# Four empty blocks in a weight stream, shorter DMA rows for the weight sums, and two ScalarE instructions exchanged

## The chip, the cores and the metric

The kernel runs on one core of one Trainium2 chip. The metric is the device time of one execution in microseconds, as the median of the runs. The profile shows one further execution of the same program, taken with the hardware profiler; its engines are PE (TensorE, with its weight loads as PEld), DVE (VectorE), ACT (ScalarE), POOL (GpSimd) and SP (SyncE, which issues the weight loads).

## The reference

Sequence length 512, width 1024, everything in float32. Two layers of a first block, then two layers of a second one:

```python
for i in range(2):                      # first block
    if i == 0:
        mix = conformer_conv(x, ...)    # x @ pw1, a * sigmoid(g), 31-tap depthwise, layer_norm, silu, @ pw2
    else:                               # 16 heads of 64
        q, k, v = x @ wq, x @ wk, x @ wv
        mix = stick_breaking_attention(q, k, v) @ wo
    x = layer_norm(alpha * x + mix)
    u = x @ w_up                        # 1024 x 2816
    g = causal_dwconv(x @ w_gate, conv_w, conv_b)      # 3 taps
    ffn = (silu(g) * u) @ w_down
    ple = sigmoid(x @ ple_gate) * (p[i] @ ple_proj)
    x = layer_norm(alpha * x + ffn + ple)
for l in range(2):                      # second block
    z = rmsnorm(x) @ w_in[l]            # split into the parts of two mixers
    x = x + concat(gated_linear_attention(z), softmax_attention(z)) @ w_out[l]
```

## The kernel before, in words

**Layout and precision.** The activations lie transposed in SBUF, as eight tiles of 128 features by 512 tokens (k = 0 to 7). To keep float32's accuracy at TensorE's faster rate, each operand is split in two: a high part, rounded to fp32r by ScalarE, and a low part, the rest, which VectorE makes by subtracting (`less`, L2192 to L2194; all its instructions carry L2194). A product of a 128x128 weight block takes three matmuls into the same bank: XH by wh, XH by wl, XL by wh (`block` in the TensorE program, its matmuls all at L620). Activations are held as `X`, `XH`, `XL`; the FFN's hidden ones as `HH`, `HL`.

**The weight stream.** All weights come as one sequence of 128x128 blocks, laid out by `weight_order` (L61) in just the order in which TensorE uses them. Eight blocks (NU = 8) make a unit of 128x1024 numbers, 512 KB; there are 308 units. SyncE loads unit after unit into a ring of three raw buffers `wraw` (`raw` in `sync_program`, L547) and reuses a buffer as soon as VectorE has made the low part of the unit three before. ScalarE rounds the unit (`round_to`, L1447) and VectorE subtracts (`rest_to`, L2198), both in strict unit order, into one of four slots `wh`, `wl`. A slot is free when TensorE has passed the last block of the unit that held it; TensorE tells this by raising the semaphore `stream` at the end of each group of blocks and at the end of each unit. Each instruction stream calls `feed` or `feed_group` at the places where TensorE uses a block; where that block is the first of a unit (p % NU == 0), the engine makes the unit three further on (AHEAD = 3). So where a unit begins in the order decides where, among an engine's other work, a rounding stands and what it waits for. Some units do not use the four slots: at four places units go into space that is free at the time (`Stream.spare`, L162 to L168), so that they can be made far ahead, beside work with which TensorE is not fed yet. For layer 1 they are the units that hold wq with k = 2, 4 and 6, for the second block's first layer those that hold in0 with k = 2, 4 and 6, in each case found by the position of that block in the sequence. `None` in the sequence is an empty block: it fills a place, is loaded with the unit, and is never multiplied.

**Start of a layer.** The normalisation of the layer before runs in two halves of the tokens, and `head` (L724) follows it: TensorE goes through k = 0 to 7 with the blocks of four output tiles for tokens 0 to 255, then again for tokens 256 to 511. For layer 1 those blocks are wq and wk of columns 0 and 1, four blocks per k, so 32 in all. At present 32 blocks do not begin at a unit's start but four blocks in: unit 117 holds the last four of layer 0 and k = 0, unit 118 k = 1 and 2, unit 119 k = 3 and 4, unit 120 k = 5 and 6, unit 121 k = 7 and the first four of wv. Units 118 to 120 are the spare ones. ScalarE rounds them between the steps of the normalisation (L1792 to L1810) and after them the unit that holds wv's first block; VectorE makes the low parts in `between_last` (L2652 to L2676), the last fill of which comes after the second half's `XL`. For in0 the sequence is aligned (`align`, L66), a spare unit holds k = 2 and 3, the next k = 4 and 5, the last k = 6 and 7, and the same code runs.

**FFN.** 22 tiles of hidden features. The first 2 * PAIRS tiles (PAIRS = (3, 7): three pairs in layer 0, seven in layer 1) are computed two at a time with a scheme that takes seven products of half size in place of eight. It needs sums of weight quarters (`tu` for up, `tg` for gate, 16 blocks a pair each) and sums of the activations (`XS`). Per pair and matrix TensorE makes the first products, then 16 summed blocks in groups of four, then the last product (`first_products`, `summed_products`, `last_product`, L792 to L819). ScalarE copies partial results out of the banks (`first_out`, `second_out`), VectorE combines them (`first_combined`, `three_combined`, `last_combined`, L2391 to L2408), and between these ScalarE and VectorE finish the pair before: VectorE's three taps of the convolution, ScalarE's `silu`, VectorE's product, the high part on ScalarE, the low part on VectorE. TensorE's last product of a pair's up matrix waits for the third value of `three_combined` (`sqr` or `third` in the rows, L2185). ScalarE's order is the loop at L1583 to L1612: silu(f - 1), which needs the taps of the pair before, then `second_out(0, tu, p)`.

**Weight sums.** POOL builds tu and tg in HBM before they are needed (`weight_sums`, L3225): each of the four parts in `SUMMED` (L25) is a chain of eight DMAs from HBM to HBM into `tw`, four copies (L3219) and four that add to what lies there (L3223). A step waits for the one before it and for a number of units made by VectorE. An entry is (layer, first and last of the matrices, that number for the first step, units between steps). Parts 0 and 1 belong to layer 0, 2 and 3 to layer 1. SyncE's loads of tu and tg blocks wait for the sums.

```python
for n, (put, dst, src) in enumerate(((copy, t3, w12), (add, t3, w22), (copy, t2, t3), (add, t2, w11),
                                     (copy, t4, t2), (add, t4, w21), (copy, t1, w12), (add, t1, w11))):
    pool.wait_ge(s.w_lo, at + step * n)
    put(dst, src, done + n)
```

**Around the change in the stream.** In `ffn_order` (L45) layer 0's pairs begin with a filler of four empty blocks for the gate blocks that a first pair doesn't have. Behind them the sequence ends layer 0 four blocks off a unit's start, so that `wq`, `wo` and layer 1's `up` begin in the middle of a unit, while layer 1's first `tu` block begins one (layer 0's first `tu` block stands in a unit's middle). The output projection takes wo with k = 0 to 4 for eight columns, then k = 5 and 6 for three columns and k = 7 last, beside the last heads of the attention (L1078 to L1090, L1888 to L1899). Unit 147 begins at the block of wo with k = 6 and column 1.

Of the kernel before, what the change touches and what calls it, by code (L numbers as in the profile page):

```python
# [5 lines left out]
ALU = mybir.AluOpType  # L6
# [15 lines left out]
ALPHA = 4.0 ** 0.25  # L22
PAIRS = (3, 7)

SUMMED = [(0, 0, 4, 16, 1), (0, 4, 6, 38, 1), (1, 0, 6, 60, 4), (1, 6, 14, 100, 5)]  # L25
XS0 = 14
TAPS = 31

# [16 lines left out]
def ffn_order(layer):  # L45
    out = []
    for p in range(PAIRS[layer]):
        f, (up, gate), (tu, tg) = 2 * p, (f"up{layer}", f"gate{layer}"), (f"tu{layer}", f"tg{layer}")
        out += [(up, k, f) for k in range(KD)]
        out += [(gate, k, f - 1) for k in range(4, KD)] if p else [None] * 4  # L50
        out += [(tu, k, p) for k in range(16)] + [(gate, k, f) for k in range(KD)]
        out += [(up, k, f + 1) for k in range(4, KD)] + [(tg, k, p) for k in range(16)]
    f = 2 * PAIRS[layer]
    out += [(f"up{layer}", k, f) for k in range(KD)] + [(f"gate{layer}", k, f - 1) for k in range(4, KD)]
    out += [(f"gate{layer}", k, f) for k in range(KD)]
    for f in range(2 * PAIRS[layer] + 1, FT):
        out += [(f"up{layer}", k, f) for k in range(KD)] + [(f"gate{layer}", k, f) for k in range(KD)]
    return out
# [1376 lines left out]
def scalar_program(act, m, s, w, nc):  # L1435
# [97 lines left out]
    def ffn(layer, i):  # L1533
        HH = m.HH[layer]
        for f0 in (0, 4):
            if f0:
                feed_group(f"pg{layer}", range(KD), range(f0, f0 + 4))
            for c in range(f0, f0 + 4):
                act.wait_ge(s.stream, w.done(f"pg{layer}", KD - 1, c))
                if c >= 4:  # L1540
                    act.wait_ge(s.pg_x, 8 * layer + c - 3)
                fn(tmp[c % 4][:, :], bank[c][:, :], ACT.Sigmoid).then_inc(s.pg_u, 1)
            if f0 == 0:
                for j in range(4):
                    act.wait_ge(s.xs_f, 4 * layer + j + 1)
                    fn(m.XS[layer][j][:, :, 0:256], m.SF[layer][j], ACT.Copy).then_inc(s.xs_h, 1)
        up, gate, tu, tg = f"up{layer}", f"gate{layer}", f"tu{layer}", f"tg{layer}"

        def bias(f, g):

            act.wait_ge(s.pg_x, 8 * layer + 8)
            if f >= 2:
                act.wait_ge(s.f_h, FT * layer + f - 1)
            fn(tmp[2 * f % 4][:, :], g[:, :], ACT.Identity, scale=P(f"fcw{layer}", 3 * f + 2), bias=P(f"fcb{layer}", f)).then_inc(s.f_u, 1)

        def silu(f):

            u = tmp[2 * f % 4]
            act.wait_ge(s.f_conv, FT * layer + f + 1)
            fn(u[:, :], u[:, :], ACT.Silu).then_inc(s.f_silu, 1)  # L1560

        def high(f):

            act.wait_ge(s.f_h, FT * layer + f + 1)
            fn(HH[:, f, :], tmp[(2 * f + 1) % 4][:, :], ACT.Copy).then_inc(s.f_hi, 1)

        def pair_bias(p, odd):
            act.wait_ge(s.u_c, combined(layer, p, 1, 4 + odd))
            bias(2 * p + odd, m.gb[odd])

        def first_out(g, mat, p):
            if g == 0 and p >= 2:
                act.wait_ge(s.f_h, FT * layer + 2 * p - 2)
            act.wait_ge(s.stream, w.done(mat, KD - 1, 2 * p))
            fn((m.ub[layer][p], m.gb)[g][0][:, 0:256], bank[3 * g][:, 0:256], ACT.Copy).then_inc(s.u_e, 1)

        def second_out(g, mat, p):
            if g == 0 and p:
                act.wait_ge(s.f_h, FT * layer + 2 * p - 1)
            act.wait_ge(s.stream, w.done(mat, 15, p))  # L1580
            fn((m.ub[layer][p], m.gb)[g][1][:, 0:256], bank[3 * g][:, 0:256], ACT.Copy).then_inc(s.u_e, 1)

        for p in range(PAIRS[layer]):  # L1583
            f = 2 * p
            if p:
                second_out(1, tg, p - 1)
            feed_group(up, range(KD), [f])
            if p:
                pair_bias(p - 1, 0)
            first_out(0, up, p)  # L1590
            if p:
                feed_group(gate, range(4, KD), [f - 1])
            feed_group(tu, range(4), [p])
            if p:
                pair_bias(p - 1, 1)
            feed_group(tu, range(4, 12), [p])
            if p:
                silu(f - 2)
            feed_group(tu, range(12, 16), [p])
            feed_group(gate, range(4), [f])  # L1600
            if p:
                silu(f - 1)
            second_out(0, tu, p)
            feed_group(gate, range(4, KD), [f])
            feed_group(up, range(4, KD), [f + 1])
            if p:
                high(f - 2)
            first_out(1, gate, p)
            feed_group(tg, range(8), [p])
            if p:  # L1610
                high(f - 1)
            feed_group(tg, range(8, 16), [p])  # L1612
        last = PAIRS[layer] - 1
        second_out(1, tg, last)
        for f in range(2 * PAIRS[layer], FT):
            feed_group(up, range(KD), [f])
            if f == 2 * PAIRS[layer]:
                pair_bias(last, 0)
                feed_group(gate, range(4, KD), [f - 1])
                pair_bias(last, 1)  # L1620
                silu(f - 2)
                silu(f - 1)
                high(f - 2)
                high(f - 1)
            feed_group(gate, range(KD), [f])
            act.wait_ge(s.stream, w.done(gate, KD - 1, f))
            bias(f, bank[gate_bank(f)])
            silu(f)
            high(f)
        table(LNEXP)  # L1630
        for c in range(7):
            feed_group(f"down{layer}", range(FT), [c])
            square(i + 1, c, X[:, c, :])
# [1569 lines left out]
def gpsimd_program(pool, m, s, a):  # L3203
    C = m.C

    def tt(o, i0, i1, op):
        return pool.e.tensor_tensor(o, i0, i1, op)

    def add_sum(i, c, x0, x):
        pool.wait_ge(s.xsum, 8 * i + c + 1)  # L3210
        if c == 1:
            pool.wait_ge(s.nrm_u, 8 * part_at(i))
        else:
            pool.wait_ge(s.accs, acc_at(i) + c - 1)
        tt(m.acc_s[:, :], x0 if c == 1 else m.acc_s[:, :], x, ALU.add).then_inc(s.accs, 1)

    def copy(dst, src, after):
        pool.wait_ge(s.tw, 16 * after)
        pool.e.dma_start(dst, src).then_inc(s.tw, 16)  # L3219

    def add(dst, src, after):
        pool.wait_ge(s.tw, 16 * after)
        pool.e.dma_start(dst, src, accum_op=ALU.add, max_dma_last_dim=8192).then_inc(s.tw, 16)  # L3223

    def weight_sums(part):  # L3225

        layer, n0, n1, at, step = SUMMED[part]
        t1, t3, t4, t2 = (a["tw"][t, layer, n0:n1].rearrange("n p c -> (n p) c") for t in range(4))
        w11, w12, w21, w22 = (a[n][layer, n0:n1].rearrange("n p c -> (n p) c") for n in ("w11", "w12", "w21", "w22"))
        done = 8 * part  # L3230
# [5 lines that stand above are left out]
    for i in (1, 3):  # L3236
        for part in ((0,), (1, 2, 3))[i // 2]:
            weight_sums(part)
        for c in range(1, KD - 1 if i == 3 else KD - TAIL[i] - SPLIT[i]):
            add_sum(i, c, m.X[:, 0, :], m.X[:, c, :])  # L3240
        for h in range(2 if SPLIT[i] else 0):
            for c in range(KD - TAIL[i] - SPLIT[i], KD - TAIL[i]):
                if h:
                    pool.wait_ge(s.xsum, 8 * i + c + 1)
                else:
                    pool.wait_ge(s.xa, half_at(i + 1) + c - KD + 1)
                pool.wait_ge(s.accs, acc_at(i) + c - 1 + (SPLIT[i] + FIRST_TAIL[i]) * h)
                v = m.acc_s[:, tokens(i, h)]
                tt(v, v, m.X[:, c, tokens(i, h)], ALU.add).then_inc(s.accs, 1)
    for layer in range(2):  # L3250
        pool.wait_ge(s.v0, layer + 1)
        for i in range(2):
            pool.e.memset(m.states[:, i, 0, :], 0.0).then_inc(s.st0, 1)
# [161 lines left out]
```

## Time and profile before

| | |
|---|---|
| runs | 1762.31, 1762.95 and 1764.30 us; median 1762.95 |
| profiled execution | 1766.01 us, its span 1764.2 us |
| granted TensorE clock, mean | 0.995 |
| busy shares | PE 98%, PEld 81%, DVE 65%, ACT 51%, POOL 2% |
| moved by DMA | 213.75 MB, 121 GB/s |

The span is what the engines' records cover; the execution's own time is 1.8 us longer. Times are counted from the start of the span. The brackets at a row give the idle time of that engine just before it and what ended it. PEclk is the clock granted to TensorE as a fraction of 2.4 GHz; 0.50 is 1.2 GHz. The stages in the trace: the convolution layer to about 230 us, layer 0's FFN behind it, layer 1 from 639 on with attention and the output projection to about 900, then its FFN with the seven pairs from about 960 to 1110, and the second block from about 1306 on.

### The profile page before, as it was taken

The numbers are of one execution on the slowest core, as the hardware profiler recorded it, in microseconds if no ns is written. First come the engines' busy times: TensorE is split into PE (matmuls) and PEld (weight loads), VectorE is DVE, ScalarE is ACT, GpSimd is POOL, SyncE is SP. The second block draws the span as 40 slices with busy tenths as digits, with TensorE's granted clock in tenths as the row PEclk, the third lists the DMA queues.
The fourth block names the chain that finished last, engine by engine and source line by source line (L and its number), as shares of the span: only waits on it lengthen the run. The fifth ranks groups of instructions, "written<-read, shape, count | busy, mean of one in ns | idle before, by whom it ended". The sixth has DMA issues, their size and how long they took to land.

```text
span 1764.2 us, 24404 instructions
## 1 busy us (share of the span) xinstructions
PE 1729.5 (98%) x9933; PEld 1436.1 (81%) x9933; DVE 1150.0 (65%) x1813; ACT 897.4 (51%) x1409; POOL 40.0 (2%) x53
## 2 busy tenths in 40 slices
PE   9999999999999979999999999999999999999999
PEld 7877998888888878777778999888898877778766
DVE  6779887644433453887687887543368866656674
ACT  6789655433332353666564565432255454534542
POOL 0000100000000000000020000000000000000000
PEclk9999999999999989999999999999999999999999
DMA  5374256755446536311114555233223222132111
GB/s 214 132 207 117 96 168 198 243 167 167 133 142 199 136 112 187 96 51 58 63 64 155 174 178 169 95 96 107 96 72 105 93 63 66 67 96 96 60 60 48
DMA packets 59808, 213.75 MB, mean 121 GB/s; under 512 B 7088, under 2 KB 7344, under 8 KB 56752
## 3 DMA queue, kind: packets, MB, share of 16 engines
q1 hardware_dynamic: 56240, 170.25, 29.4%
q0 software_dynamic: 3456, 41.95, 9.0%
q8 instruction: 78, 1.28, 0.3%
q14 instruction: 34, 0.28, 0.0%
HBM read 207.97 MB, written 44.04 MB: 143 GB/s over the span
## 4 chain that ended last, share of the span: by engine, by line
PE 79%; DVE 10%; ACT 6%; DMA 2%; issue 2%; SPq 0%; ACTq 0%; DVEq 0%
PE bank L620 78%; DVE tmp L2185 3%; DVE wl L2194 2%; ACT tmp L1439 2%; ACT wh L1439 1%; DMA wraw<-in_wstream 1%; DMA wraw<-tw 1%; DVE XL L2194 1%; ACT taps L1439 1%; DVE tmp L2182 1%; DVE HL L2194 1%; DVE sqr L2185 1%; PE bank L1384 0%; ACT X L1439 0%; DVE HH L2194 0%
## 5 line engine op out<-in xcount | busy, mean ns | idle before, releaser
L2194 DVE TENSOR_TENSOR wl<-wraw,wh 128x1024 fp32r<-128x1024 f32 (+1 forms) x295 | 357.4, 1220 | 304.6 <-ACT wh L1439 303.5
L620 PE MATMUL bank<-XH,wh 128*128 128x512 f32 (+1 forms) x1424 | 527.9, 371 | 14.2 <-DVE wl L2194 11.8
L620 PE MATMUL bank<-XL,wh 128*128 128x512 f32 (+1 forms) x1424 | 517.7, 364 | 0.0
L620 PE MATMUL bank<-XH,wl 128*128 128x512 f32 (+1 forms) x1424 | 517.7, 364 | 0.0
L1439 ACT ACTIVATE wh<-wraw 128x1024 fp32r<-128x1024 f32 (+1 forms) x295 | 309.1, 1054 | 362.2 <-PE bank L620 318.4
L620 PEld LDWEIGHTS bank<-XH,wh 128*128 128x128 f32 x1424 | 269.7, 189 | 67.9 <-issue 20.2
L620 PEld LDWEIGHTS bank<-XH,wl 128*128 128x128 f32 x1424 | 269.6, 189 | 43.1
L620 PEld LDWEIGHTS bank<-XL,wh 128*128 128x128 f32 x1424 | 270.0, 190 | 39.6 <-issue 0.7
L620 PE MATMUL bank<-HL,wh 128*128 128x256 f32 (+1 forms) x740 | 215.4, 333 | 9.2 <-DVE sqr L2185 7.9
L620 PE MATMUL bank<-HH,wh 128*128 128x256 f32 (+1 forms) x740 | 216.2, 334 | 0.1
L620 PE MATMUL bank<-HH,wl 128*128 128x512 f32 (+1 forms) x580 | 199.8, 345 | 0.0
L620 PEld LDWEIGHTS bank<-HL,wh 128*128 128x128 f32 x740 | 130.2, 192 | 24.7 <-DVE sqr L2185 9.4
L620 PEld LDWEIGHTS bank<-HH,wh 128*128 128x128 f32 x740 | 130.0, 191 | 14.1 <-DVE Y L2185 0.6
L620 PEld LDWEIGHTS bank<-HH,wl 128*128 128x128 f32 x580 | 110.4, 190 | 13.1
L1439 ACT ACTIVATE tmp<-tmp 128x512 f32<-128x512 f32 (+2 forms) x131 | 72.1, 591 | 66.1 <-DVE tmp L2182 65.6
L1439 ACT ACTIVATE tmp<-bank 128x512 f32<-128x512 f32 (+4 forms) x129 | 70.3, 566 | 16.1 <-PE bank L620 14.0
L2185 DVE TENSOR_TENSOR X<-X,bank 128x512 f32<-128x512 f32 (+1 forms) x58 | 38.5, 666 | 41.8 <-PE bank L620 41.7
L2182 DVE SCALAR_TENSOR_TENSOR tmp<-bank,prm,tmp 128x511 f32<-128x511 f32 (+1 forms) x48 | 35.9, 749 | 44.3 <-ACT tmp L1439 43.5
L1439 ACT ACTIVATE tmp<-bank,prm 128x512 f32<-128x512 f32 (+1 forms) x44 | 30.5, 696 | 56.3 <-PE bank L620 56.0
L620 PE MATMUL bank<-XH,HL 128*128 128x256 f32 x256 | 57.6, 287 | 0.3 <-DVE XL L2194 0.2
L620 PE MATMUL bank<-wh,XH 128*128 128x512 f32 x128 | 50.7, 396 | 0.1
L1439 ACT ACTIVATE sqr<-X 128x512 f32<-128x512 f32 (+1 forms) x41 | 23.2, 567 | 52.7 <-DVE X L2185 48.4
(383 smaller groups left out, 2438.9 us busy)
## 6 DMA issues: line engine op xcount, KB each, us to landing
wraw<-in_wstream SPq DMA_DIRECT2D x257, 512.0 KB, 3.6
wraw<-tw SPq DMA_DIRECT2D x80, 256.0 KB, 3.0
tw<-in_w POOLq DMA_DIRECT2D x6, 1536.0 KB, 10.9
tw<-in_w POOLq DMA_DIRECT2D x4, 2048.0 KB, 16.4
wraw<-in_wstream SPq DMA_DIRECT2D x22, 256.0 KB, 3.1
tw<-in_w POOLq DMA_DIRECT2D x4, 1024.0 KB, 10.5
tw<-in_w POOLq DMA_DIRECT2D x6, 512.0 KB, 6.7
tw<-tw POOLq DMA_DIRECT2D x2, 1536.0 KB, 7.9
```

Of the source, the lines that this page charges most:

```text
L620: return pe.e.matmul(o, l, r, start=start, stop=stop, skip_group_check=True)
L1439: return act.e.activation(o, i, f, **kw)
L2182: return dve.e.scalar_tensor_tensor(out=o, in0=i0, scalar=sc, in1=i1, op0=op0, op1=op1)
L2185: return dve.e.tensor_tensor(o, i0, i1, op)
L2194: return dve.e.tensor_tensor(o, x, h.bitcast(F32), ALU.subtract)
```

## The change

The gate blocks of the first tile behind the pairs are followed by four empty blocks, in both layers. The stream becomes 309 units long (2472 blocks, with 2464 before), and every block behind layer 0's pairs moves by four, every block behind layer 1's pairs by eight in all. In the ScalarE program's loop over the pairs the copy of the second product is put ahead of silu(f - 1). The weight sums' DMAs, copies and adds, get rows of at most 4096 bytes (max_dma_last_dim; the adds had 8192, the copies none), and parts 0 and 1 of the weight sums begin one and two units earlier.

```diff
--- before.py
+++ after.py
@@ -22,7 +22,7 @@
 ALPHA = 4.0 ** 0.25
 PAIRS = (3, 7)
 
-SUMMED = [(0, 0, 4, 16, 1), (0, 4, 6, 38, 1), (1, 0, 6, 60, 4), (1, 6, 14, 100, 5)]
+SUMMED = [(0, 0, 4, 15, 1), (0, 4, 6, 36, 1), (1, 0, 6, 60, 4), (1, 6, 14, 100, 5)]
 XS0 = 14
 TAPS = 31
 
@@ -52,7 +52,7 @@
         out += [(up, k, f + 1) for k in range(4, KD)] + [(tg, k, p) for k in range(16)]
     f = 2 * PAIRS[layer]
     out += [(f"up{layer}", k, f) for k in range(KD)] + [(f"gate{layer}", k, f - 1) for k in range(4, KD)]
-    out += [(f"gate{layer}", k, f) for k in range(KD)]
+    out += [(f"gate{layer}", k, f) for k in range(KD)] + [None] * 4
     for f in range(2 * PAIRS[layer] + 1, FT):
         out += [(f"up{layer}", k, f) for k in range(KD)] + [(f"gate{layer}", k, f) for k in range(KD)]
     return out
@@ -1598,9 +1598,9 @@
                 silu(f - 2)
             feed_group(tu, range(12, 16), [p])
             feed_group(gate, range(4), [f])
+            second_out(0, tu, p)
             if p:
                 silu(f - 1)
-            second_out(0, tu, p)
             feed_group(gate, range(4, KD), [f])
             feed_group(up, range(4, KD), [f + 1])
             if p:
@@ -3216,11 +3216,11 @@
 
     def copy(dst, src, after):
         pool.wait_ge(s.tw, 16 * after)
-        pool.e.dma_start(dst, src).then_inc(s.tw, 16)
+        pool.e.dma_start(dst, src, max_dma_last_dim=4096).then_inc(s.tw, 16)
 
     def add(dst, src, after):
         pool.wait_ge(s.tw, 16 * after)
-        pool.e.dma_start(dst, src, accum_op=ALU.add, max_dma_last_dim=8192).then_inc(s.tw, 16)
+        pool.e.dma_start(dst, src, accum_op=ALU.add, max_dma_last_dim=4096).then_inc(s.tw, 16)
 
     def weight_sums(part):
```

## Rows read from the trace of the kernel before

**Rows 1.** Page, part 1: busy time, share of the span, instructions of each engine.

```profile
PE 1729.5 (98%) x9933; PEld 1436.1 (81%) x9933; DVE 1150.0 (65%) x1813; ACT 897.4 (51%) x1409; POOL 40.0 (2%) x53
```

**Rows 2.** Timeline of PE (start us, us, instruction, [idle before <-releaser]), start of layer 1.

```profile
638.92 0.55 PE L620 MATMUL bank<-XH,wh 128*128 128x256 f32 x1 [9.95 <-DVE wl L2194]
```

**Rows 3.** Timeline of PE, four of the pairs' last products.

```profile
289.55 0.80 PE L620 MATMUL bank<-HL,wh 128*128 128x256 f32 x2 [3.70 <-DVE sqr L2185]
...
984.42 0.50 PE L620 MATMUL bank<-HL,wh 128*128 128x256 f32 x2 [1.42 <-DVE sqr L2185]
...
1005.44 0.50 PE L620 MATMUL bank<-HL,wh 128*128 128x256 f32 x2 [0.61 <-DVE third L2185]
...
1089.57 0.50 PE L620 MATMUL bank<-HL,wh 128*128 128x256 f32 x2 [0.61 <-DVE sqr L2185]
```

**Rows 4.** Timeline of ACT and PE, output projection of layer 1.

```profile
877.89 1.06 ACT L1439 ACTIVATE wh<-wraw 128x1024 fp32r<-128x1024 f32 x1 [6.70 <-PE bank L620]
...
880.86 0.50 PE L620 MATMUL bank<-OH,wh 128*128 128x512 f32 x1 [1.71 <-DVE OL L2194]
```

**Rows 5.** Convolution stage: its window (columns under Rows 7), and a row of ACT's timeline.

```profile
100.00:200.00 100.00, 96.27 (x709) 80.94 (x708) 83.51 (x132) 83.02 (x136) 11.09 (x12) 1.00 0.54 160
...
114.02 1.06 ACT L1439 ACTIVATE HH<-wraw 128x1024 fp32r<-128x1024 f32 x1 [3.24 <-DMA wraw<-in_wstream]
```

**Rows 6.** Timeline of ACT and DVE, start of layer 1 (x3: merged with two rows behind).

```profile
631.74 1.04 ACT L1439 ACTIVATE wh<-wraw 128x1024 fp32r<-128x1024 f32 x1
...
637.55 3.49 DVE L2194 TENSOR_TENSOR wl<-wraw,wh 128x1024 fp32r<-128x1024 f32 x3
```

**Rows 7.** Windows: busy us of PE, PEld, DVE, ACT, POOL; PEclk, DMA share, GB/s.

```profile
630.00:640.00 10.00, 1.08 (x5) 1.11 (x6) 8.46 (x19) 8.37 (x15) 0.00 (x0) 0.65 0.02 6
...
640.00:650.00 10.00, 10.00 (x74) 10.00 (x74) 1.04 (x1) 0.00 (x0) 0.00 (x0) 0.84 0.42 153
...
1306.00:1310.00 4.00, 3.68 (x28) 3.37 (x27) 3.91 (x9) 3.46 (x8) 0.00 (x0) 1.00 0.33 129
```

**Rows 8.** Chain of waits (start us, us, what).

```profile
260.78 7.69 DMA wraw<-in_wstream
...
274.26 8.18 DMA wraw<-tw
...
880.86 16.99 PE bank L620 x70
...
1005.44 14.68 PE bank L620 x120
```

**Rows 9.** Windows, attention stage of layer 1.

```profile
700.00:800.00 100.00, 99.16 (x574) 75.28 (x573) 81.99 (x172) 69.83 (x139) 0.89 (x1) 1.00 0.26 71
```

**Rows 10.** Timeline of ACT and DVE, third pair of layer 1.

```profile
1003.57 0.63 ACT L1439 ACTIVATE tmp<-tmp 128x512 f32<-128x512 f32 x1 [0.46 <-DVE tmp L2182]
...
1004.11 0.37 ACT L1439 ACTIVATE third<-bank 128x256 f32<-128x256 f32 x1
...
1004.51 0.42 DVE L2185 TENSOR_TENSOR sqr<-third,bank 128x256 f32<-128x256 f32 x1 [0.97 <-ACT third L1439]
```

**Rows 11.** DMA view of 220 to 290 us (queue: packets, MB, share); last row: whole kernel.

```profile
q0 software_dynamic: 448, 4.19, 23.5%
...
wraw<-in_wstream SPq DMA_DIRECT2D x6, 512.0 KB, 4.8
...
wraw<-in_wstream SPq DMA_DIRECT2D x257, 512.0 KB, 3.6
```

**Rows 12.** Timeline of POOL: two issues of the weight sums.

```profile
247.54 0.78 POOL L3223 DMA_DIRECT2D tw<-in_w  x1 [8.25 <-DVE wl L2194]
...
273.64 0.78 POOL L3223 DMA_DIRECT2D tw<-in_w  x1 [4.48 <-DMA tw<-in_w]
```

**Rows 13.** Windows, PE alone (busy us, PEclk, DMA share, GB/s), behind the 3.70 us.

```profile
290.00:294.00 4.00, 4.00 (x21) 0.50 0.41 134
...
294.00:298.00 4.00, 4.00 (x31) 0.87 0.80 239
```

## The prediction

> **What bounds the kernel now.** I read the page's busy shares first: TensorE's matmuls fill 1729.5 us, 98% of the span [rows 1]. The change adds and removes no matmul, so only the 34.7 us in which PE is idle can move, and what PE loses at half clock after an idle stretch. The next view is PE's timeline, searched for rows with idle time in brackets. One is large: 9.95 us before 638.92 [rows 2]. The others within reach are 3.70 before 289.55, 1.42 before 984.42 and 0.61 or 0.62 before each of five pairs from 1005.44 to 1089.57 [rows 3], 1.71 before 880.86 [rows 4], and 3.73 in all between 100 and 200 us [rows 5]. The question at each is which wait ends last, and whether the change touches it.
>
> **The padding, at the head of layer 1.** The stream stands four blocks off there: units 118 to 120 are the spare ones, rounded early, but wq and wk of k = 7 stand in unit 121, with wv 0. PE goes through k = 0 to 7, first for tokens 0 to 255. VectorE makes unit 121's low part only after the whole normalisation (the last fill of `between_last`): at 637.55, its high part having been made at 631.74 [rows 6]. So PE stops at 629, at k = 7 of the first half. With four blocks of padding 118 is an ordinary unit and 119 to 121 are the spare ones with k = 2 to 7. That is the order which the in0 stage has today, in the same code: there PE is busy 3.68 of 4 us where its normalisation starts [rows 7], 0.32 lost. The second half's XL rows come late, but they end by 637.6 [rows 6]; a k takes PE twelve matmuls of 0.122 (120 in 14.68 us [rows 8]), 1.46 us, and starting the second half at about 630 it reaches k = 7 at 640. Nothing is late next. Gain: 9.95, and the clock. PEclk 0.84 over 640 to 650 is 3.2 us at 1.2 GHz in place of 2.4 [rows 7]; with the 1.08 before 640 that is 4.3 us at half speed, 2.1 lost. **12.0 us**, bounds 8 and 12.3.
>
> **The padding, elsewhere.** The stream grows from 308 to 309 units: one more load and rounding, 1.04 us of ScalarE and 1.16 of VectorE [rows 6], beside PE, 0. If that cover is gone they cost 2.2 once. In the attention stage ScalarE's rounding moves from k = 4 of a matrix to k = 0, ahead of the next scores. PE is busy 99.16 of 100 us there [rows 9]. I take 0, with bounds of one rounding, -1 and +1.
> In the output projection unit 147 starts now at wo 6,1. ScalarE's round for it waits until PE has finished wo 6,0, and it stands ahead of the last head's copy: it comes at 877.89 after 6.70 us of idle time, and PE waits 1.71 for OL [rows 4]. After the shift the unit starts at wo 5,0 and the round waits for wo 4,7, four blocks earlier, twelve matmuls of 0.24 (70 in 16.99 [rows 8]), 2.9 us, more than the stall. **1.7**, bounds 0 and 1.7.
> From layer 1's own padding on, the stream is today's moved by a whole unit: 0.
>
> **The second copy ahead of the second silu.** In each pair ScalarE runs silu(f-1), which waits for VectorE's taps, at 1003.57, and then the copy of the second product at 1004.11; VectorE's three combinations follow from 1004.51 [rows 10], and PE's last product starts at 1005.44 when the second one is done. That second product was finished long before: eight blocks of 0.37 lie between it and the waiting one. Copied first, it lets the combinations start when the taps end, at about 1003.55, 1.0 us sooner. The stall is 0.61, so all of it goes; five times, and the 1.42 of the second pair, where ScalarE also loads a table: 4.5. silu(f-1) slips by the copy, 0.37 [rows 10]; behind it VectorE's product and the high part are wanted only a pair later. Layer 1's pairs also get layer 0's alignment, in which no unit starts at gate k = 0, so that one feed less stands between. **4.3**, bounds 2.5 and 4.7.
>
> **The weight sums and layer 0's pairs.** The 3.70 us before 289.55 come from loads: in the chain of waits stand a load of 7.69 us at 260.78 and one of 8.18 at 274.26 [rows 8]; the median is 3.6 over the kernel and 4.8 in this stretch [rows 11]. Beside them run POOL's sums, step 3 of part 1 at 247.54 and step 7 at 273.64, 6.5 us a step [rows 12], in packets of 9.4 KB (4.19 MB in 448 [rows 11]). With the threshold two units lower, step 5 stands where step 3 did and step 7 at 260.6: this traffic ends near 267, not 280. The load at 274 then costs what the median does, 4.6 less, and with the reorder's 1.0 the chain through load, table, silu and taps is early enough. PE gains 3.70, and the clock behind it: PEclk 0.50 and 0.87 [rows 13] with the 0.45 before 290 are 5.5 us at 1.2 GHz, 2.7 lost at most. Bounds: 1.0 (the reorder alone) and 6.4. Nearest is layer 1's second pair, without sums beside it, which loses 1.42 in the old order and less than the reorder and alignment give back in the new one. **5.4**.
> No row prices the shorter rows. A load meets packets of 9.4 KB now; at 4 KB its wait for a turn should halve. Against it, queue 0's packets more than double; if each cost what it does now, its share of 23.5% [rows 11] would pass 50%. Their own effect lies between -2 and +2 us.
> The Trainium skill's page "DMA: Bandwidth & Descriptors" (Queues, rings and completion order) says that an engine takes turns between queues by whole packets of several descriptors. By that rule shorter rows give nothing unless the packet shrinks with them; the sum would be 1.4 us smaller. No row here tells a packet from a descriptor.
> In the convolution stage ScalarE, which paces it, waited 3.24 us for a load at 114.02 [rows 5], while part 0 moves its data. PE's 3.73 us of idle time hang on ScalarE. Part 0 starts a unit earlier, which shifts its steps against the loads and doesn't clear them. Bounds -2 and 3.0; **1.4**, for the shorter turns.
>
> **Sum.** 12.0 + 1.7 + 4.3 + 5.4 + 1.4 = 24.8 us. The profiled execution took 1766.0 (span 1764.2), 3.1 over the median of the runs, 1762.95. Against it this is 1741.2, against the median **1738**.
>
> **Rivals.**
> *The DMA parts give nothing:* the earlier sums meet other loads. Against it: they do leave 267 to 280. Then 1.4 goes and 5.4 becomes 1.0: 24.8 - 5.8 = 19.0, **1744**.
> *Row size is indifferent, only the thresholds work* (the packet rule's case): 1.4 goes and a third of layer 0's: 21.6, **1741**.
> *The head of layer 1 keeps part of its wait:* XL's second half or wv's first unit ends last in place of unit 121; 3 to 5 us stay with some of the clock, **1743**. Against it: the in0 stage.
> *Slower:* the sums come too late. Layer 0's third pair reads part 1. A pair takes 21.0 us ((1089.57 - 1005.44) / 4 [rows 3]), its sums are multiplied from the middle on and loaded three units (8.8 us) ahead, so none is wanted before about 289.55 + 10.5 - 8.8, say 290. Three steps remain after 247.54: done at 267, 23 us to spare. It bites when smaller rows double a step to 14 us; at 24 us a step the sums end at 319.5, PE waits 29.5, and the kernel takes 1738 + 29.5 = **1767.5**. Packets that each cost what they do now would make a step at most 2.3 times as long (9.4 / 4), 15 us, and the sums end at 292.5, 2.5 late.
> *It doesn't do what it says:* the spare units could fall on other blocks and unit 121's wait stay. Worked out from the order, they move along.
>
> **Numbers.** Forecast 0.60 (its own range 1733 to 1742), no gain from DMA 0.14, rows indifferent 0.12, part of the head's wait left 0.09, slower 0.03, nothing 0.02. All but the last two are faster: 0.95. A measurement of this kernel tells 0.2%, 3.5 us, from no change. Range 1733 to 1746: the low end has 3.0 in the convolution stage, 6.4 in layer 0 and one rounding in attention (24.8 + 1.6 + 1.0 + 1.0, and the shorter rows' own 1.6 at most); the high end is the first rival with two roundings in the way.
>
> **What would show it.** Right: no idle row of 10 us near 630; PE's last product of layer 1's pairs without idle time from the third on, the copy to `third` or `sqr` ahead of the silu; no idle time before wo 7; POOL's last add of part 1 at about 260; loads beside the sums at 3 to 4 us; over 10,000 packets on queue 0. Wrong: a new PE row waiting for wl behind DMA wraw<-tw, half clock anywhere between 300 and 1700, sums of part 1 ending after 290. The forecast falls if the head of layer 1 isn't shorter by 11 us or more, for that is half of the sum.

## The result and the profile after

The changed kernel took 1736.62 us (median of four runs, 1735.42 to 1736.95), the kernel before 1762.63 beside it; the ratio is 0.9851, with a 95% interval of 0.9838 to 0.9863. That is 26.0 us less. The forecast was 1738 (24.8 us less), in a range of 1733 to 1746. The same kernel in a later set of runs took 1740.04 (below, the run of the change again), so the eight runs together have a median of 1736.9.

The page after: the busy shares, the granted clock in 40 slices, and the DMA queues.

```profile
span 1735.0 us, 24407 instructions
...
PE 1722.2 (99%) x9933; PEld 1430.8 (82%) x9933; DVE 1149.9 (66%) x1814; ACT 898.0 (52%) x1410; POOL 42.7 (2%) x53
...
PEclk9999999999999999999999999999999999999999
...
q1 hardware_dynamic: 56384, 170.77, 30.2%
q0 software_dynamic: 10752, 41.95, 9.6%
...
wraw<-in_wstream SPq DMA_DIRECT2D x258, 512.0 KB, 3.6
```

As many matmuls as before [rows 1], PE's busy time 7.3 us shorter, the span 29.2 us shorter. The 7.3 are put down to what the idle stretches had cost in clock and in pipelining, since the matmuls are the same. Queue 0, on which the weight sums run, has three times its packets for the same bytes.

PE's timeline after, the rows with idle time between 200 and 1300 us (the rows left out between them have no idle time).

```profile
206.36 0.38 PE L620 MATMUL bank<-XH,HL 128*128 128x256 f32 x1 [0.20 <-DVE XL L2194]
...
264.68 0.50 PE L620 MATMUL bank<-HL,wh 128*128 128x256 f32 x2 [1.39 <-DVE sqr L2185]
...
609.80 0.39 PE L620 MATMUL bank<-XH,wh 128*128 128x256 f32 x1 [0.25 <-DVE XL L2194]
...
688.17 0.50 PE L620 MATMUL bank<-XH,wh 128*128 128x512 f32 x1 [0.30 <-DVE OH L2182]
...
816.87 0.50 PE L620 MATMUL bank<-OH,wh 128*128 128x512 f32 x1 [0.26 <-DVE X L2182]
...
837.82 0.50 PE L620 MATMUL bank<-OH,wh 128*128 128x512 f32 x1 [0.26 <-DVE X L2182]
...
1278.25 0.39 PE L620 MATMUL bank<-XH,wh 128*128 128x256 f32 x1 [0.32 <-DVE XL L2182]
```

The 9.95 us of [rows 2], the 3.70, 1.42 and five times 0.6 of [rows 3] and the 1.71 of [rows 4] have no counterpart. All idle rows of PE together fall from 30.9 us to 9.2. One row is worse: 1.39 at 264.68, where the kernel before had 0.51.

Windows after (busy us of PE, PEld, DVE, ACT, POOL; PEclk, DMA share, GB/s): layer 1's start, what follows layer 0's third pair, and 100 us of attention, which answer to [rows 7], [rows 13] and [rows 9].

```profile
620.00:630.00 10.00, 10.00 (x86) 10.00 (x85) 8.49 (x23) 8.82 (x18) 0.00 (x0) 1.00 0.01 2
284.00:288.00 4.00, 4.00 (x36) 4.00 (x35) 4.00 (x7) 3.36 (x6) 0.00 (x0) 1.00 0.20 71
690.00:790.00 100.00, 100.00 (x588) 76.56 (x587) 81.20 (x170) 69.21 (x140) 1.16 (x1) 1.00 0.28 74
```

PE's granted clock is 1.00 there: 36 matmuls in 4 us behind the third pair, where there were 21 and 31.

ScalarE and VectorE in layer 1's third pair after, to be held against [rows 10], and POOL's last step of part 1, against [rows 12].

```profile
977.26 0.38 ACT L1439 ACTIVATE third<-bank 128x256 f32<-128x256 f32 x1 [0.38 <-PE bank L620]
977.67 0.42 DVE L2185 TENSOR_TENSOR sqr<-third,bank 128x256 f32<-128x256 f32 x1
977.76 0.63 ACT L1439 ACTIVATE tmp<-tmp 128x512 f32<-128x512 f32 x1
978.13 0.42 DVE L2185 TENSOR_TENSOR third<-bank,sqr 128x256 f32<-128x256 f32 x1
```

```profile
260.16 0.81 POOL L3223 DMA_DIRECT2D tw<-in_w  x1 [3.95 <-DMA tw<-in_w]
```

The copy to `third` stands ahead of the silu, the combinations begin with no idle time when the taps end (977.67), and the one that PE wants is done at 978.55, 1.3 us before PE's last product at 979.88. The last step of part 1 lands 8.44 us after its issue, at 268.6.

ScalarE's rounding ahead of the last head's copy, against [rows 4]:

```profile
852.69 1.06 ACT L1439 ACTIVATE wh<-wraw 128x1024 fp32r<-128x1024 f32 x1 [2.40 <-PE bank L620]
```

**Where the 29.2 us of the two spans went.** The same row of PE is found in both timelines, and the difference of the start times is read: 0.4 us is gained by 9.7 us (before the sums begin), 1.2 by 207, 7.1 at 617 (609.80), 19.7 at 708 (688.17), 20.5 at 837 (816.87), 29.2 at 1307 (1278.25) and at the end. So: start and convolution 1.2, layer 0's FFN 5.9, layer 1's start 12.1 with 0.5 of the first attention stall behind it, the rest of attention 0.7, and 8.7 from there to the second block. The profiled execution of before stood 3.4 us over the median beside it (1766.0 and 1762.63), that of after 0.2 over its own; this is why 29.2 us of span are 26.0 in the medians. From the row at 617 to the end it is 1147.3 us before and 1125.2 after, 22.1 less, and 1125.2 to 1126.2 in all nine profiles that have the padding. What lies ahead of that row differs from execution to execution, as the experiments show.

### The profile page after: what moved, and what is told of

It reads as the page before. It is cut to its first block, busy times and chain, and to the rows that moved or that the text cites. A ratio compares the mean times of both kernels' runs of the same rounds, so it can differ in the third digit from the quotient of the medians.

```text
span 1735.0 us, 24407 instructions
## 1 busy us (share of the span) xinstructions
PE 1722.2 (99%) x9933; PEld 1430.8 (82%) x9933; DVE 1149.9 (66%) x1814; ACT 898.0 (52%) x1410; POOL 42.7 (2%) x53
## 3 DMA queue, kind: packets, MB, share of 16 engines
q0 software_dynamic: 10752, 41.95, 9.6%
## 4 chain that ended last, share of the span: by engine, by line
PE 89%; DVE 5%; ACT 4%; DMA 1%; issue 1%; SPq 0%; DVEq 0%; ACTq 0%
PE bank L620 88%; ACT tmp L1439 1%; DMA wraw<-in_wstream 1%; DVE wl L2194 1%; DVE tmp L2185 1%; ACT wh L1439 1%; ACT taps L1439 1%; PE bank L1384 0%; DVE XL L2194 0%; DVE sbl L2194 0%; DVE HL L2194 0%; ACT Y L1439 0%; ACT XH L1439 0%; DVE X L2182 0%; DVE sqr L2185 0%
## 5 line engine op out<-in xcount | busy, mean ns | idle before, releaser
L620 PE MATMUL bank<-wh,XL 128*128 128x512 f32 x128 | 49.9, 390 | 0.0
```

The costliest lines, as they stand in the source:

```text
L620: return pe.e.matmul(o, l, r, start=start, stop=stop, skip_group_check=True)
```

## The experiments

Twelve runs of kernels (the ninth is the change itself), in three sets of four, each set on a chip of its own; each set shares its runs of the kernel before. The first four take the change apart.

**e1, the padding alone.** The `[None] * 4` of the diff and nothing else.

> The padding alone, everything else as before. The idle 9.95 us at layer 1's start and its half clock (12.3 us together by the two profiles) and the 1.71 us ahead of wo with k = 7 go; of layer 1's pairs the theory, which gives their gain to the exchange of the copy and silu, expects the stalls to stay at 0.5 to 0.7 us each: 12.3 + 1.5 = 13.8 us, ratio 0.9922. Rival: the shift of unit starts alone clears the pairs' stalls (before, a unit starts at the gate's k = 0, ahead of the copy): 13.8 + 6.4 = 20.2 us, ratio 0.9885. Layer 0's pairs and the convolution stage lie ahead of the padding: nothing there by either.

Measured: 1740.4 us (1738.69 to 1745.68) against 1762.61, ratio 0.9883 (0.9866 to 0.99): 22 us by the medians, 21 by the ratio. The rival holds. PE's timeline, the last product of layer 1's second pair and of the third:

```profile
962.48 0.51 PE L620 MATMUL bank<-HL,wh 128*128 128x256 f32 x2 [0.40 <-DVE sqr L2185]
...
982.74 0.40 PE L620 MATMUL bank<-HL,wh 128*128 128x256 f32 x2
```

The third has no idle time, with silu still ahead of the copy. ScalarE has silu at 980.62, the copy at 981.16, and the combinations start at 981.56. From silu's start to PE's turn it is 2.1 us, where it was 1.1 before (1003.57 [rows 10] to 1004.67): the order is the old one, and it is a microsecond earlier against PE. Where the microsecond comes from stands in VectorE's timelines, before (first row) and with the padding alone (second row). It is the low part that VectorE makes ahead of the product and the taps for which silu waits:

```profile
1000.26 1.23 DVE L2194 TENSOR_TENSOR wl<-wraw,wh 128x1024 fp32r<-128x1024 f32 x1 [1.16 <-ACT wh L1439]
...
977.32 1.23 DVE L2194 TENSOR_TENSOR wl<-wraw,wh 128x1024 fp32r<-128x1024 f32 x1 [0.57 <-ACT wh L1439]
```

It starts 4.4 us ahead of PE's turn before and 5.4 with the padding. Its rounding, the one that ScalarE does ahead of silu(f - 2), had waited 0.48 us for PE (999.17), and with the unit starting four blocks earlier it waits for PE no more (976.24). The rounding at the gate's k = 0 (1002.05) was not what held silu back before: it had ended 0.46 us earlier [rows 10].

**e2, the exchange alone.**

```diff
+            second_out(0, tu, p)
             if p:
                 silu(f - 1)
-            second_out(0, tu, p)
```

> The exchange of copy and silu alone. Theory: 0.6 to 0.8 us in each of layer 1's pairs from the third on and 1 us of the second pair's 1.42, about 4.5 us, and 1.0 us or more in layer 0's third pair, with what of the clock comes back: 5 to 8 us in all, ratio 0.9955 to 0.997. Rival (a unit starts at the gate's k = 0 with the old alignment, and its rounding still stands ahead of the copy and waits for a bank or a load): the stalls stay, 0 to 1 us. Second rival for layer 0: its 3.70 us come from silu's table and taps, and the copy alone clears them, then PE shows no half clock at 290 though the sums still run late.

Measured: 1755.72 us (1754.84 to 1759.1) against 1762.61, ratio 0.997 (0.9959 to 0.9981): 5 to 7 us, the theory's own case. PE's timeline, layer 0's second pair, layer 1's second, and layer 1's third:

```profile
266.37 0.80 PE L620 MATMUL bank<-HL,wh 128*128 128x256 f32 x2 [3.49 <-DVE sqr L2185]
...
978.50 0.50 PE L620 MATMUL bank<-HL,wh 128*128 128x256 f32 x2 [0.36 <-DVE sqr L2185]
...
998.76 0.40 PE L620 MATMUL bank<-HL,wh 128*128 128x256 f32 x2
```

Layer 1's stalls go here too. From the first pair's last product to the seventh's it is 127.0 us in the kernel before (962.58 to 1089.57), 121.6 with the padding alone, 121.7 with the exchange alone and 121.0 with both. **The two edits cure the same stall**: 5.4 and 5.3 alone, 6.0 together. In layer 0 a stall of 3.49 stands at the second pair in place of the third: it wanders from execution to execution.

**e3, the shorter rows alone**, and **e4, the lower thresholds alone** (both as in the diff).

> Rows of 4096 bytes alone, thresholds as before. Theory (a load waits for the turn of a packet of the sums, and this one is half as long): loads beside the sums go from 4.7 to below 4 us in the median, the convolution stage gains 1 us, layer 0's third pair 1 to 3 us: 1 to 4 us, ratio 0.998 to 0.9995. Rival (only when the sums run matters, not how their rows are cut): the medians stay at 4.7 us and the ratio is 0.9995 to 1.0005. Packets on queue 0 are near 10,750 by both.

> Thresholds of parts 0 and 1 lower by one and two units alone. Theory: part 1 ends near 267 us in place of 280, the loads at 274 cost their median and layer 0's third pair loses at most 1 us in place of 3.70, with the clock behind it 3 to 6 us gained; convolution stage within 0.5 us: ratio 0.9965 to 0.998. Rival (the reorder or the rows are needed for it): under 1 us, ratio above 0.9994.

Measured: rows 1762.75 us (1760.73 to 1767.63), ratio 1.0008 (0.9997 to 1.0018); thresholds 1761.73 us (1758.39 to 1766.96), ratio 0.9996 (0.9985 to 1.0006). Neither is told from no change; the medians of the times are those of the rivals (the rows' ratio lies just past its 1.0005). The single profiles say more. DMA view of 220 to 290 us, thresholds alone, and PE's row at layer 0's third pair:

```profile
wraw<-in_wstream SPq DMA_DIRECT2D x6, 512.0 KB, 3.9
```

```profile
284.78 0.50 PE L620 MATMUL bank<-HL,wh 128*128 128x256 f32 x2 [0.40 <-DVE sqr L2185]
```

And with the rows alone:

```profile
wraw<-in_wstream SPq DMA_DIRECT2D x6, 512.0 KB, 4.4
```

```profile
271.74 0.50 PE L620 MATMUL bank<-HH,wh 128*128 128x256 f32 x2 [1.27 <-DVE acc_s L2185]
...
289.54 0.80 PE L620 MATMUL bank<-HL,wh 128*128 128x256 f32 x2 [3.15 <-DVE sqr L2185]
```

The median load (of six) is 3.9 and 4.4 us, against 4.8 [rows 11], and the stall of 3.70 becomes 0.40 and 3.15. What the thresholds gain in layer 0 in this profile (403.3 us from PE's row at 207 to that at 617, 409.3 before) the timed runs don't show in full; why, the later sets tell in part.

**e5, one unit earlier, without padding.** ScalarE rounds unit 121 behind the first half's last tile, VectorE subtracts it there:

```diff
-            elif h == 1 and f == 3:
+            elif h == 0 and f == 7:
                 round_to(w.at["wv", 0, 0] // NU)
...
                 between(i, mat, t)
+                if i == 2 and t == 7:
+                    rest_to(w.at["wv", 0, 0] // NU)
```

> The stream as before, without padding; only unit 121 (wq and wk of k = 7, wv 0) is rounded and subtracted earlier, behind the first half's normalisation in place of after the second. Theory (PE's 9.95 us wait for that one unit's low part): PE then has k = 7 at about 630 us, the idle row falls under 1 us and the clock stays up, 11 to 12.3 us gained, ratio 0.993 to 0.994, while the stalls of wo and of layer 1's pairs stay as they were. Rival (the second half's XL or a later unit ends next): 3 to 5 us stay, gain 5 to 8 us, ratio 0.9955 to 0.997.

Measured: 1751.8 us (1750.66 to 1754.06) against 1762.74, ratio 0.9938 (0.9926 to 0.9951): 11 us. VectorE's timeline and the window in which PE had been busy for 1.08 us before [rows 7]:

```profile
627.26 1.22 DVE L2194 TENSOR_TENSOR wl<-wraw,wh 128x1024 fp32r<-128x1024 f32 x1
```

```profile
630.00:640.00 10.00, 10.00 (x86) 10.00 (x85) 8.53 (x20) 8.38 (x15) 0.00 (x0) 1.00 0.14 50
```

So the stall at layer 1's start hangs on one unit's low part, 1.22 us of VectorE's work 10 us too late, and PE has no idle row of 0.2 us or more from there to 695.70. From 616.66 to the first attention stall (695.70) it is 79.0 us, 91.0 before, 78.4 with the padding. The other stalls (0.84, 0.99, 1.71, and 0.6 in the pairs) are all in this trace, at their old size: they don't hang on unit 121. The first three are in e2's trace too, so of the change's parts only the padding can have taken them.

**e6, the change without the exchange**, and **e7, the change without both edits of the sums.**

> The change without the exchange of copy and silu. If the shifted unit starts clear layer 1's pairs by themselves, as the run with padding alone says, only layer 0's third pair can lose something: 1737 to 1739 us, ratio to before 0.9855 to 0.9865. If the exchange is worth what the prediction gives it (4.3 us in layer 1): 1741 us, ratio 0.988.

> The change without shorter rows and earlier thresholds: padding and exchange alone. The prediction's sum without its 1.4 us of the convolution stage and with 1.0 in place of 5.4 in layer 0's pairs would be 1742.4. By the single runs of rows and thresholds (within 0.2% of before) it is 1736 to 1739 us, ratio 0.985 to 0.9865, with a wider spread of the runs than the change's own 1.5 us, since loads meet the sums at other moments each time.

Measured: 1740.31 us (1738.72 to 1744.65), ratio 0.9875 (0.9859 to 0.9892), and 1740.83 us (1738.89 to 1741.6), ratio 0.9873 (0.9859 to 0.9886). Both lie between the two values expected of each, and about 4 us over the change's first; whether that is the parts or the set of runs, e9 was to tell. In e6 the stretch from 837 to the second block takes 462.1 us, 461.4 in the change: the exchange is worth 0.7 us in layer 1 once the padding is in, not the 4.3 of the prediction.

**e8, a version beyond the change.** In layer 0's second pair the copy waits behind a rounding, and the rounding for a load. The copy is put ahead of it:

```diff
                 silu(f - 2)
+            second_out(0, tu, p)
             feed_group(tu, range(12, 16), [p])
             feed_group(gate, range(4), [f])
-            second_out(0, tu, p)
```

> The change, and the copy of the up matrix's second product put ahead of the rounding at the summed block 12 too, where in layer 0's second pair the copy waits for a rounding that waits for a load (the change's profile loses 1.39 us there at 264.68). Theory: that stall goes, 0.5 to 1.4 us gained in layer 0, layer 1 as it was: 1735.5 to 1736.5 us, ratio to before 0.985. Rival: the rounding behind the copy comes late by the copy's wait and PE waits for its low part: a new row waiting for wl in each pair, 0.5 us or more times ten, 1741 us.

Measured: 1739.94 us (1738.69 to 1740.99), ratio 0.9871 (0.9856 to 0.9887): not the 1735.5 to 1736.5 of the theory. PE waits for no wl in any pair, and layer 0 from 209.65 to 611.58 takes 401.9 us, the shortest of all profiles. But the convolution stage lost it again, to a load of 8.75 us at 121.32 in the chain of waits:

```profile
134.64 0.80 PE L620 MATMUL bank<-cinh,HH 32*128 32x512 f32 x4 [4.20 <-DVE cinl L2194]
```

**e9, the change again**, the scale for the three that follow.

> The changed kernel once more, so that the next three runs can be held against it on the same chip. In the runs of the change on record it took 1735.4 to 1737.0 us; other chips gave 1739 to 1741 for kernels that lack one part each. If those parts are worth what lies between, this one comes to 1736.6 again; if it is the chip or the day, it comes to 1738 to 1740 and the three parts (exchange, both of the sums' edits) are worth 1 to 2 us at the most.

Measured: 1740.04 us (1736.67 to 1743.26) against 1761.99, ratio 0.9879 (0.9858 to 0.9899). The same program, and its runs spread over 6.6 us. So e6, e7 and e8 can't be told from the change by their medians, and neither can the padding alone: e1's 22.2 us and 0.9883 stand beside 22.0 and 0.9879 here. What the exchange and the sums add to the padding is seen in the profiles and in the change's first four runs, not in this set. Its profiled execution took 1743.3, 6.4 us more than the change's first; of these 2.9 arise before the row at 207, 3.4 between it and the row at 617, 0.1 behind. Two rows of PE carry it, with ScalarE's wait in front of the second.

```profile
134.54 0.80 PE L620 MATMUL bank<-cinh,HH 32*128 32x512 f32 x4 [3.72 <-DVE cinl L2194]
...
269.65 0.80 PE L620 MATMUL bank<-HL,wh 128*128 128x256 f32 x2 [3.41 <-DVE sqr L2185]
```

```profile
260.92 0.82 POOL L3223 DMA_DIRECT2D tw<-in_w  x1 [4.68 <-DMA tw<-in_w]
261.04 0.80 SPq L561 DMA_DIRECT2D wraw<-tw  x2
...
267.36 1.06 ACT L1439 ACTIVATE wh<-wraw 128x1024 fp32r<-128x1024 f32 x1 [7.15 <-DMA wraw<-tw]
268.32 0.37 ACT L1439 ACTIVATE sqr<-bank 128x256 f32<-128x256 f32 x1
```

POOL issues the last sum of part 1 at 260.92, SyncE a unit's loads 0.12 us later, and ScalarE gets that unit after 7.15 us; the copy stands behind the rounding, and PE waits 3.41. Loads of such length stood in the chain of [rows 8] too. From layer 1's start on nothing of the kind is seen: the stretch from 617 to 837 takes 207.0 to 207.1 us in all nine profiles with the padding, and the one from 1307 to the end 456.7 to 456.8 in all fourteen.

**e10, part 0 at its old threshold; e11, the change with the old rows; e12, e8 with part 0 at its old threshold.**

> The change, but part 0 of the weight sums at its old threshold (16); part 1 keeps the new one (36). By the profiles so far layer 0's pairs take 403 to 404 us from 207 on with the lower thresholds and 407 to 410 without, and the stretch up to 207 takes 206.4 to 209.7 with them and 204.1 to 207.6 without. Theory: part 1's threshold gives all of the gain in layer 0 and part 0's costs something in the convolution stage, where it starts earlier and ends among the same loads: 0.5 to 2 us less than the change. Rival: part 0's place is indifferent and the differences up to 207 us are chance: within 0.5 us of the change.

> The change with the rows of the sums' DMAs as before (8192 bytes in the adds, uncut in the copies). Theory, by the run of rows alone (1.0008 of before, 0.9997 to 1.0018): the row size is indifferent, within 1 us of the change. Rival (shorter rows help only once the sums are moved): 1 to 3 us slower than the change, in the convolution stage, with the loads' median beside the sums above 4.6 us.

> A version meant to beat the change: the copy of the second product ahead of the rounding at summed block 12, and part 0 of the sums at 16. The copy alone took layer 0's pairs from 403.4 to 401.9 us by the profiles. Theory: 1.5 us from that, and what part 0's old threshold gives (0 to 2 us): 1.5 to 3 us below the change. Rival: the differences are lost in the spread of the loads, within 1 us of the change.

Measured, against 1761.99: e10 1739.51 us (1735.35 to 1741.99), 0.9873 (0.9851 to 0.9896); e11 1739.84 us (1737.01 to 1744.04), 0.988 (0.9859 to 0.9901); e12 1736.78 us (1735.97 to 1737.11), 0.9859 (0.9842 to 0.9877). The old rows cost nothing that shows beside e9. Part 0's threshold is not told apart by the runs. e12 is 3.3 us under e9 in the median and its runs keep within 1.1 us; the intervals overlap, and the change's own first runs had a median within 0.2 us of it (1736.62), so it isn't shown to beat the change. Its profile speaks against a version without late loads: ScalarE waits 5.51 us for a load before 267.52, PE 1.78 for `acc_s` at 270.23, and layer 0 takes 403.9 us, where 401.9 were expected from e8.

**All fourteen profiles together** say what single medians can't (the fourteenth is the kernel before). From PE's row at about 207 us to that at about 617:

| thresholds of the sums | layer 0's FFN, us | mean |
|---|---|---|
| part 1 at 38 (before, e1, e2, e3, e5, e7) | 409.3, 407.4, 406.8, 408.7, 410.3, 407.8 | 408.4 |
| part 1 at 36 (change, e4, e6, e8 to e12) | 403.4, 403.3, 404.0, 401.9, 406.8, 403.8, 402.9, 403.9 | 403.8 |

Up to the row at 207 us it takes 206.0 in the mean of the eight profiles with part 0 at 16 (204.1 to 207.6), and 207.7 in the mean of the six with part 0 at 15 (206.4 to 209.7). Part 1's earlier start gives 4.6 us, with one exception among fourteen (e9, for the reason above, which reaches the lowest of the other row); part 0's seems to cost 1.7, in ranges that overlap. Together 2.9 us; the timed runs of e4 gave 0.7, with an interval that reaches to 2.6 and takes in no gain at all. Between e7, which lacks both edits of the sums, and the change it is 0.8 by the second set of runs and 4.2 by the first. The size of the sums' part thus stays open between nothing and some 4 us.

## Why the prediction was right, and where not

**The head of layer 1: right.** 12.0 us forecast, 12.1 by the two timelines, 11 in e5's medians for the unit alone. The step "that is the order which the in0 stage has today" carried it: 0.32 us are lost at in0 [rows 7], and from 609.80 to 688.17 PE has no idle row at all. The second half's XL did not end last; the rival fell.

**The output projection: right.** 1.7 forecast; from PE's row before it (857.79 and 837.82) to the one at the old stall (880.86 and 859.04) the difference grows by 1.85. ScalarE's rounding is 5.2 us earlier against PE than before (852.69 and 877.89, with 19.97 between the two timelines), more than the 2.9 of the prediction.

**The pairs of layer 1: the mechanism was right, the term too small and given to the wrong edit.** "The stall is 0.61, so all of it goes; five times": the six periods fell by 6.0 us and not by 4.3, beyond the bound of 4.7. A bracket of 0.61 isn't what a stall costs. PE issues a matmul of this form every 0.12 us, while the row shows 0.28 for each; ahead of 1005.44 the last one starts at 1004.55, so the next is 0.77 late against its turn, and the pair's first weight block loses another 0.10. The period falls from 21.03 to 20.16, by 0.87 for 0.61 of idle time. And the alignment, which the sentence on it counts as one feed less, was worth the whole: either edit alone gives nearly all. It works by another unit than the prediction names: not by the feed at gate k = 0, but by the rounding and low part ahead of the taps, which come a microsecond earlier (e1). Counted one after the other, the exchange adds 0.7 behind the padding.

**Attention: taken at 0.** It gave 0.5 and 0.7 at the first stalls (0.84 to 0.30, 0.99 to 0.26) and lost 0.5 at a new one at 837.82, so 0.7 net, within the bounds of 1. That the padding moves these stalls is shown: the nine profiles with it have the new sizes, e5 and the others without it the old ones. That ScalarE's rounding at k = 0 in place of k = 4 is the reason is argued only.

**Layer 0 and the weight sums: the mechanism is borne out by the profiles, the size open.** "This traffic ends near 267": the last add stands at 260.16 and lands at 268.6, and PE's stall at layer 0's third pair is 0.53 us at the most in the eight profiles with the lower threshold, and 1.16 to 4.41 in five of the six without it (e2 has none). 5.4 forecast, 5.9 between the two profiles, 4.6 from the thresholds by all profiles, 0.7 from e4's timed runs. The exchange's 1.0 is neither shown nor refuted: without the lower thresholds e2 and e7 average 407.3 and the four others 408.9, in ranges that overlap. Its working at the stall held as well: from 271 us, where the two timelines differ by 0.8, to 295, where they differ by 7.1, it is 6.3 us for a stall of 3.70 and the clock behind it, against 6.4 at most. What the step missed is the second pair: there the copy is behind a rounding that is behind a load, hence 1.39 at 264.68 and 3.41 in e9. The move of the sums didn't bring this about. Before, a step stood at nearly the same time (260.81), and e2 and e1, with the old thresholds, lose 3.49 and 1.38 at the second pair.

**The convolution stage: not supported.** "1.4, for the shorter turns": the profiles' 1.2 up to 207 us have 0.4 before the sums begin, and shorter rows change nothing in e3 (1.0008) and e11 (0.988 beside 0.9879). Part 0's earlier start has, if anything, the other sign. The rival "row size is indifferent, only the thresholds work" is what the runs support; its price was small.

**The sum: near in part by luck.** Against the profiled execution it said 1741.2; after took 1736.8. Of the 4.4 us between, layer 1's pairs are 2.4 (1.7 in the six periods, 0.7 at the first pair's 0.47, which had no term), attention 0.7, layer 0 0.5, the output projection and the wl row behind it 0.4; the rest is under 0.5. Against the medians the sum is 1.2 us short, since before's profiled execution was a long one and the sum took its stalls as typical. Two errors of opposite sign also meet in it. From 617 us on the terms come to 18.0 (12.0, 1.7 and 4.3), where all profiles with the padding show 21 to 22; ahead of that they come to 6.8 (5.4 and 1.4), of which the timed runs of rows and thresholds alone show next to nothing. The change's second set, 22.0 us under before, fits 22 from layer 1 on and almost nothing ahead of it; the first set, 26.0, had more ahead. Both lie in the range.

**The slower rival** wanted a step of 24 us; after, part 1's copies and adds land in 4.3 and 7.4 us in the median beside layer 0's FFN and end near 267, far from 290.

## What to carry to other kernels

When a stream of fixed units feeds an engine, look at which unit the first consumer of a stage stands in: four blocks in the wrong unit cost 12 us here, and a few empty blocks, or that unit made earlier (11 us), bring it back. Before two edits are summed, ask whether they cure the same wait; test each alone and look at the same row. Look also at what stands behind an instruction that waits for a load: a short copy there made PE wait 1.39 us in one execution of this kernel and 3.41 in another. With the copy put first one profile had no such stall (e8), another had one by a different path (e12), so the remedy isn't shown. And where single executions differ by more than an edit is worth, hold the stretch that the edit can touch against the same stretch in many profiles.

## What the runs showed of the hardware

Cutting the sums' rows to 4096 bytes raised queue 0's packets from 3456 to 10752 for the same 41.95 MB, and its share of the DMA engines from 9.0% to 9.6% only: the time of what the profile counts as a packet went nearly with its bytes, and the fear that each would cost what it did before (a share past 50% in layer 0) fell. DMA view of 220 to 290 us after, to be held against [rows 11]:

```profile
q0 software_dynamic: 864, 3.15, 18.6%
...
wraw<-in_wstream SPq DMA_DIRECT2D x6, 512.0 KB, 3.6
```

The Trainium skill's page "DMA: Bandwidth & Descriptors" (Queues, rings and completion order) has an engine drain a whole packet before it turns to another queue. By that rule shorter packets should shorten the loads' wait. What the profile counts as a packet did shrink, to 3.9 KB (41.95 MB in 10752), about one row of 4096 bytes; whether the page's packet, which holds several descriptors, shrank with it no run here shows, so the rule is not tested. The loads beside the sums went from 4.8 to 4.4 us with the rows alone [rows 11], to 3.9 with the thresholds alone, in the median of six; in time nothing came of the rows. A 512 KB or 256 KB load of the stream takes from 3.2 to 8.8 us between 220 and 290 us of this one execution, and nothing here says what decides it.

PE's granted clock in the 4 us behind an idle stretch in layer 0's pairs: 0.50 behind 3.70 us [rows 13], 0.66 behind the 3.41 us at 269.65 in e9, 0.60 behind 2.08 us at 269.54 in e7, 1.00 behind 1.78 us at 270.23 in e12 and behind the 1.39 us at 264.68 in the change. Window of PE in e9 behind that row:

```profile
270.00:274.00 4.00, 4.00 (x25) 0.66 0.39 139
```

So the two long stretches cost more than their idle time, 6.3 us for 3.70 and 12.1 for 9.95, with half clock behind them; the 1.39 us brought no loss of clock.
